# Loading weights one block earlier around the branch mixing of a transformer block

## The chip, the cores and the metric

The kernel runs on one core of a Trainium2 chip. The metric is the device time of one execution in microseconds (us). The kernel computes two transformer blocks over 512 tokens of width 1024, all in float32; this change touches the first block only, between its stick-breaking attention and its first residual addition.

## The reference

What is computed in the part that matters, from `first_block`:

```python
mod = jax.nn.silu(c) @ ada_w[layer] + ada_b[layer]
shift1, scale1, gate1, shift2, scale2, gate2 = [m[:, None, :] for m in jnp.split(mod, 6, axis=-1)]
...
y_a = nsa_attention(...) @ w_up_nsa[layer]                     # 512x512 times 512x1024
y_b = stick_breaking_attention(...) @ w_up_sb[layer]           # 512x512 times 512x1024
mixed = (jax.nn.sigmoid(m_a) * y_a + jax.nn.sigmoid(m_b) * y_b) @ w_out[layer]
h = h + gate1 * mixed
u2 = rms_norm(h, norm2_g[layer]) * (1 + scale2) + shift2
```

`w_up_nsa` and `w_up_sb` (2 MB each) are called the branch weights here, `w_out` (4 MB) the output weight. `ada_w` has 6 x 1024 columns; `gate1`, `scale2`, `shift2` and `gate2` are not computed ahead of this part but beside it.

## The kernel before

The program is a list of blocks. In each `nc.Block()` every engine has its own instruction list; engines meet by semaphores inside a block, and all of them, SyncE (SP) with its DMA issues included, meet in a barrier at its end. SP need not wait for the data of a DMA, only until it has issued it. Scratch memory is a stack from the left (`Scope(nc)`) and one from the right (`beside`).

The blocks around the change, in order:

1. `stick_breaking` (L1366): 8 heads; TensorE, VectorE and ScalarE hand each other the scores. SP has nothing to do in it, and no DMA runs. Its result is in `mT[:, 4:8, :]`, used as `B.oT[1]`.
2. `turn_tokens` with tag `oT` (L2943, function L1509): 4 jobs in which TensorE turns the other branch's output and VectorE (even jobs) or ScalarE (odd jobs) copy it to `oT0`. SP runs `load_up` (L2937): both branch weights into `wu`, units 0 and 1 of the modulation, then two rows of biases (`load_biases`, L154), 512 KB each, one row of 4 KB spread to all 128 partitions.
3. `mix_branches` (L1553): 8 parts, each 128 tokens by 512 columns. A part is 8 matmuls in the code (4 slices of 128 for each of the two branches); the trace has two MATMUL records for each, 16 a part. TensorE starts part i when VectorE has read part i-2 (`read`). VectorE multiplies both banks by the gates `B.sig` (L1593 into `mixed`, L1594 into a scratch tile), GpSimd adds the two (L1607).
4. `turn_tokens` with tag `mT` (L2946): 8 jobs, `mixed` turned into `mT`.
5. `project_residual` (L1610) with tag `o1`: 8 groups of 16 MATMUL records, two halves of `w_out` in `rw0` and `rw1`, both issued by SP at the start of the block (L1634). VectorE multiplies by the gate (L1676), GpSimd adds to `h` (L1693).

The modulation (`class Modulation`, L115) runs inside blocks 3 and 5. It has 8 units of 2 MB of `ada_w`, two buffers `adaw0`, `adaw1`. A unit is: a load (`load_unit`, L162; from unit 2 on it waits until the sum of the unit two before is done), a `sum` on VectorE (1 instruction at L174, 7 at L176, each waiting for the one before), a `spread` on TensorE (2 records at L188 for a gate, 8 at L195 for a scale or shift), and a `finish` on VectorE (L205, L217 or L221 and L222). In `mix_branches` VectorE does unit i//2's `sum` after an even part i and its `finish` after the odd part; TensorE does its `spread` after the odd part, and waits there for the sum. SP issues the loads of units 2 to 5 in `mix_branches`, ScalarE those of 6 and 7 in `project_residual`. Units 4 to 7 are summed in `project_residual`.

Of the kernel before, what the change touches and what calls it, by code (L numbers as in the profile page):

```python
# [22 lines left out]
P = 128  # L23
TOK = 512
NT = TOK // P
D = 1024
# [1336 lines left out]
KEY_OFF = [0, 512, 1024, 896]  # L1363


def stick_breaking(nc, C, B):  # L1366

    with Scope(nc) as s:  # L1370
# [17 lines left out]
            return tile[:, KEY_OFF[b]:KEY_OFF[b] + TOK - P * b]  # L1388

        with nc.Block() as block:  # L1390
            @block.tensor
            def _(pe):
                def scores(n):
                    i, half = n // 2, n % 2
                    r = slice(64 * half, 64 * half + 64)
                    if n >= 2:
                        pe.wait_ge(wgt_ready, 2 * (n - 1))
                    for b in (1, 3, 2, 0):
                        dst = z[half][KEY_BANK[b]][:, KEY_COL[b]:KEY_COL[b] + TOK - P * b]
                        nc.tensor.matmul(dst, B.sbk[r, i, P * b:P * b + P], B.sbq[r, i, P * b:TOK], start=(b != 3), stop=False)  # L1400
                    for b in (1, 3, 2, 0):
                        dst = z[half][KEY_BANK[b]][:, KEY_COL[b]:KEY_COL[b] + P]
                        mm = nc.tensor.matmul(dst, C.ident_r[:, :], C.ban_turned[:, :], start=False, stop=(b != 1))
                        if b != 1:
                            mm.then_inc(z_ready, 1)

                def sums(n):
                    half = n % 2
                    pe.wait_ge(plus_ready, 3 * n + 2)
                    for b in (3, 2, 1, 0):  # L1410
                        if b == 0:
                            pe.wait_ge(plus_ready, 3 * n + 3)
                        bank, col = z[half][KEY_BANK[b]], KEY_COL[b]
                        for a in range(b, NT):
                            first = col + P * (a - b)
                            mm = nc.tensor.matmul(bank[:, first:first + TOK - P * a],
                                                  (C.tri_neg if a == b else C.ones_neg)[:, :], block_of(soft[half], a),
                                                  start=False, stop=(a == NT - 1), skip_group_check=True)
                        if b < 2:
                            mm.then_inc(exponent_ready, 1)  # L1420

                def weigh(n):
                    i, half = n // 2, n % 2
                    pe.wait_ge(wgt_ready, 2 * n + 2)
                    if half == 0 and i >= 2:
                        pe.wait_ge(out_copied, i - 1)
                    for b in range(NT):
                        mm = nc.tensor.matmul(ops[i % 2][64 * half:64 * half + 64, P * b:TOK],
                                              B.sbv[:, b, n * 64:n * 64 + 64], block_of(wgt[half], b),
                                              start=(b == 0), stop=(b == NT - 1), skip_group_check=True)  # L1430
                    mm.then_inc(weighed, 1)

                scores(0)
                scores(1)
                for n in range(0, heads, 2):
                    sums(n)
                    sums(n + 1)
                    for half in range(2):
                        weigh(n + half)
                        if n + 2 < heads:  # L1440
                            scores(n + 2 + half)
# [108 lines left out]
                                         scale=1.0 if scale is None else scale).then_inc(out[1], 1)  # L1550


def mix_branches(nc, B, wu, w_in, mixed, mod):  # L1553


    with Scope(nc) as s:
        tmp = [s.sb(f"mixt{i}", [P, 512]) for i in range(2)]
        ps = [[s.bank(f"mx{i}{b}") for b in range(2)] for i in range(2)]
        ready = s.sem("mx_ready")
        own = s.sem("mx_own")  # L1560
        read = s.sem("mx_read")
        summed = s.sem("mx_sum")
        parts = [(t, n) for n in range(2) for t in range(NT)]
        with nc.Block() as block:
            @block.sync
            def _(sp):
                for u in range(2, 6):
                    mod.load_unit(sp, u)

            @block.tensor  # L1570
            def _(pe):
                for i, (t, n) in enumerate(parts):
                    if i >= 2:
                        pe.wait_ge(read, i - 1)
                    for b in range(2):
                        if i == 0:
                            pe.wait_ge(w_in[b], 16)
                        for k in range(4):
                            mm = nc.tensor.matmul(ps[i % 2][b][:, :], B.oT[b][:, k, P * t:P * t + P],
                                                  wu[b][:, k, 512 * n:512 * n + 512], start=(k == 0), stop=(k == 3))  # L1580
                    mm.then_inc(ready, 1)
                    if i % 2:
                        mod.spread(pe, i // 2)

            @block.vector
            def _(dve):
                ch = Chain(dve, own)
                for i, (t, n) in enumerate(parts):
                    dve.wait_ge(ready, i + 1)
                    dst = mixed[:, t, 512 * n:512 * n + 512]  # L1590
                    if i >= 2:
                        dve.wait_ge(summed, i - 1)
                    ch.link(nc.vector.tensor_tensor(dst, ps[i % 2][0][:, :], B.sig[:, t, 512 * n:512 * n + 512], ALU.mult))  # L1593
                    ch.link(nc.vector.tensor_tensor(tmp[i % 2][:, :], ps[i % 2][1][:, :],  # L1594
                                                    B.sig[:, t, D + 512 * n:D + 512 * n + 512], ALU.mult))
                    dve.sem_inc(read, 1)
                    if i % 2 == 0:
                        mod.sum(dve, i // 2)
                    else:
                        mod.finish(dve, i // 2)  # L1600

            @block.gpsimd
            def _(pool):
                for i, (t, n) in enumerate(parts):
                    pool.wait_ge(read, i + 1)
                    dst = mixed[:, t, 512 * n:512 * n + 512]
                    pool.tensor_tensor(dst, dst, tmp[i % 2][:, :], ALU.add).then_inc(summed, 1)  # L1607


def project_residual(nc, C, aT, w, gate, tag, mod, begun, after, early):  # L1610

# [1 line left out]
    kc = w.shape[0] // P  # L1615
    slots = kc // KD
    with Scope(nc) as s:
        wbuf = [s.sb(f"rw{i}{tag}", [P, KD, 512]) for i in range(2)]
        tmp = [s.sb(f"rt{i}{tag}", [P, 512]) for i in range(2)]
        banks = [s.bank(f"rp{b}{tag}") for b in range(6)]  # L1620
        units = len(mod.units)
        landed = s.sems(f"r_landed{tag}", 2)
        used = s.sem(f"r_used{tag}")
        ready = s.sem(f"r_ready{tag}")
        scaled = s.sem(f"r_scaled{tag}")
# [1 line left out]
        with nc.Block() as block:  # L1627
            @block.sync
            def _(sp):
                for i in range(2 * slots):  # L1630
                    if i >= 2:
                        sp.wait_ge(used, i - 1)
                    n, q = i // slots, i % slots
# [1227 lines left out]
def program(nc, A, out):  # L2861

    Scope.used.clear()
    with Scope(nc) as s:
# [25 lines left out]
        with Scope(nc, "right") as beside, Scope(nc) as s0:  # L2890
# [4 lines left out]
            with Scope(nc) as s1:  # L2895
# [4 lines left out]
                with Scope(nc) as s1b:  # L2900
# [3 lines left out]
                    with Scope(nc) as s2:  # L2904
# [16 lines left out]
                        for tag, kz, branch in (("sl", B.ksz, 1), ("wn", B.kwz, 2)):  # L2921
# [5 lines left out]
                                bias=lambda half, i: C.bias[:, bass.ds(i + 4 * half, 1), :].rearrange("p a n -> p (a n)"),  # L2927
                                gate=lambda half, i: B.ga[:, :, bass.ds(i * 3 + 12 * half + branch, 1)].rearrange("p t a -> p (t a)"),
                                add=True)
                    stick_breaking(nc, C, B)  # L2930
                mod = Modulation(beside, nc, C, M[0], C.cols1, A["ada_w"][0], A["ada_b"][0], [2, 4, 3, 5], "m2")
                with Scope(nc) as s1c:
                    B.oT[0] = s1c.sb("oT0", [P, 4, TOK])
                    wu = [s1c.sb(f"wu{i}", [P, 4, D]) for i in range(2)]
                    w_in = s1c.sems("up_in", 2)

                    def load_up(sp):  # L2937
                        for b, n in enumerate(("w_up_nsa", "w_up_sb")):
                            sp.dma_start(wu[b][:, :, :], A[n][0].rearrange("(k p) n -> p k n", p=P)).then_inc(w_in[b], 16)
                        for u in range(2):  # L2940
                            mod.load_unit(sp, u)
                        mod.load_biases(sp)
                    turn_tokens(nc, C, [(lambda t, k=k: B.oa[:, t, P * k:P * k + P], B.oT[0][:, k, :], None)  # L2943
                                        for k in range(4)], "oT", load_up, back_to_front=True)
                    mixed = s1c.sb("mixed", [P, NT, D])
                    mix_branches(nc, B, wu, w_in, mixed, mod)  # L2946
                    turn_tokens(nc, C, [(lambda t, k=k: mixed[:, t, P * k:P * k + P], mT[:, k, :], None)
                                        for k in range(KD)], "mT")
            project_residual(nc, C, mT, A["w_out"][0], M[0].gate[0], "o1", mod, 4, lambda u: u - 2, 6)
        Scope.clear(nc)  # L2950

        with Scope(nc) as s1:
# [123 lines left out]
```

## Time and profile before

| | us |
|---|---|
| median of 3 runs | 2178.98 |
| lowest and highest of them | 2174.85, 2180.03 |
| the profiled execution | 2174.3 |
| its span | 2172.5 |
| TensorE busy | 1766.9 (81%) |
| VectorE busy | 757.5 (35%) |
| ScalarE busy | 483.4 (22%) |
| GpSimd busy | 219.2 (10%) |

A row of the timeline is: start, length, engine, line of the kernel, instruction, tile written and tiles read, shapes, count, and in brackets how long the engine had been idle before it and what released it. Rows with a count above 1 are merged, and the length is then from the first start to the last end. PE is TensorE's matmul, DVE VectorE, ACT ScalarE, POOL GpSimd; SPq and PEq are the instruction queues of SyncE and TensorE, and "PEq L1515" as a releaser is the barrier that closes a block. A row of the windows is: stretch and its length, busy time with count for PE, PEld, DVE, ACT and POOL, then the mean granted TensorE clock (1.00 is 2.4 GHz, 0.50 is 1.2 GHz), the mean busy share of the DMA engines, and GB/s.

### The profile page before, as it was taken

Reading aid. Unit: us, or ns where it says so; the run is one execution under the profiler, and the core shown is the slowest. Engines: PE = TensorE matmul, PEld = TensorE weight load, DVE = VectorE, ACT = ScalarE, POOL = GpSimd, SP = SyncE. Lnnn points to the kernel's source line nnn. Section 1 sums busy time; section 2 is a strip of 40 time slices with the busy share of each in tenths; the row PEclk is TensorE's granted clock in tenths of the full one; section 3 lists DMA queues with packets and bytes.
Section 4 is the critical chain, followed back from the end, with each engine's and each line's share of the span. In section 5 each row is a group of like instructions: output and inputs, shape, how many; then the busy total and the mean of one; then the engine's idle time right before and its main releaser. Section 6 shows DMA issues by size and latency. Waiting matters only on the chain. (4 is left out here: it accounts for less than half of the span.)

```text
span 2172.5 us, 21463 instructions
## 1 busy us (share of the span) xinstructions
PE 1766.9 (81%) x8022; PEld 1177.2 (54%) x8023; DVE 757.5 (35%) x1353; ACT 483.4 (22%) x804; POOL 219.2 (10%) x261
## 2 busy tenths in 40 slices
PE   4979998887877899899959993688458889988872
PEld 2768876654344678678848881466423233323331
DVE  6334225431544677233351215643231111111113
ACT  3212334432001222222232324242100001100001
POOL 4010001000102122200030000101010000000001
PEclk9989999888989899999979995898568999999997
DMA  9312310002461775222212210004539966799994
GB/s 281 109 58 78 97 40 1 0 0 103 158 223 39 249 252 195 98 77 95 95 43 88 88 58 1 0 25 177 228 149 426 423 265 257 312 426 426 425 424 169
DMA packets 99668, 361.52 MB, mean 166 GB/s; under 512 B 21239, under 2 KB 23459, under 8 KB 87275
## 3 DMA queue, kind: packets, MB, share of 16 engines
q1 hardware_dynamic: 90791, 344.48, 41.8%
q0 software_dynamic: 5760, 9.02, 1.2%
q10 hardware_dynamic: 3012, 6.59, 0.8%
q8 instruction: 69, 1.13, 0.2%
q14 instruction: 36, 0.29, 0.0%
HBM read 357.28 MB, written 14.75 MB: 171 GB/s over the span
## 5 line engine op out<-in xcount | busy, mean ns | idle before, releaser
L2288 PE MATMUL x_gpa<-x_ring,x_Ta 128*64 128x512 f32 x608 | 136.2, 601 | 1.6 <-issue 1.6
L2288 PE MATMUL x_upa<-x_ring,x_Ta 128*64 128x512 f32 x608 | 133.7, 592 | 1.7 <-DMA x_ring<-in_w_expert_up_dram 1.7
L2288 PEld LDWEIGHTS x_gpa<-x_ring,x_Ta 128*64 128x64 f32 x608 | 43.7, 139 | 90.6 <-issue 90.6
L317 DVE TENSOR_TENSOR p_lo<-p_raw,p_hi 128x2048 fp32r<-128x2048 f32 x18 | 41.3, 2292 | 144.9 <-ACT p_hi L670 144.9
L2288 PEld LDWEIGHTS x_upa<-x_ring,x_Ta 128*64 128x64 f32 x608 | 43.6, 137 | 88.9 <-issue 88.9
L324 PE MATMUL fr_p<-p_hi,u_high 128*128 128x512 f32 x224 | 89.1, 398 | 0.0
L2272 PE MATMUL x_t0a<-ident,x_ga 128*128 128x128 f32 x80 | 20.3, 401 | 84.4 <-DMA x_ga<-normed_rows,x_idsa 84.4
L326 PE MATMUL fr_p<-p_hi,u_low 128*128 128x512 f32 x224 | 88.0, 393 | 0.0
L325 PE MATMUL fr_p<-p_lo,u_high 128*128 128x512 f32 x224 | 88.0, 393 | 0.0
L2309 PE MATMUL x_y0a<-x_ring,x_aTa 128*64 128x512 f32 x304 | 78.8, 665 | 1.2 <-ACT x_aTa L2349 1.2
L2309 PE MATMUL x_y1a<-x_ring,x_aTa 128*64 128x512 f32 x304 | 68.4, 592 | 0.0
L2272 PEld LDWEIGHTS x_t0a<-ident,x_ga 128*128 128x128 f32 x80 | 13.4, 207 | 101.0 <-DMA x_ga<-normed_rows,x_idsa 97.7
L670 ACT ACTIVATE p_hi<-p_raw 128x2048 fp32r<-128x2048 f32 (+1 forms) x20 | 37.4, 1872 | 135.5 <-DMA p_raw<-in_w_in_dram 135.5
L176 DVE SCALAR_TENSOR_TENSOR acc1m<-adaw1m,silu_c,acc1m 128x512 f32<-128x512 f32 x70 | 65.4, 934 | 2.5
L2344 ACT ACTIVATE x_siga<-x_gpa 128x512 f32<-128x512 f32 x19 | 11.3, 597 | 243.2 <-PE x_gpa L2288 243.2
L2763 POOL TENSOR_TENSOR hT<-hT 128x512 f32<-128x512 f32 x32 | 48.1, 1502 | 170.1 <-ACT hT L2753 167.3
L2358 DVE TENSOR_TENSOR x_outa<-x_y0a,gates 128x512 f32<-128x512 f32 x19 | 13.1, 691 | 147.4 <-PE x_y1a L2309 147.4
L324 PE MATMUL mp<-uh,w_hi0m 128*128 128x512 f32 x128 | 52.8, 413 | 13.6 <-DVE w_lo0m L317 13.6
L2349 ACT ACTIVATE x_aTa<-x_apa 128x512 f32<-128x512 f32 x19 | 11.3, 597 | 227.5 <-PE x_apa L2296 227.5
L317 DVE TENSOR_TENSOR w_lo0o<-w_raw0o,w_hi0o 128x2048 fp32r<-128x2048 f32 x10 | 22.9, 2292 | 109.9 <-ACT w_hi0o L2810 109.9
L2318 DVE TENSOR_SCALAR x_Ta<-x_t0a,scale,shift 128x128 f32<-128x128 f32 x80 | 27.4, 404 | 84.7 <-PE x_t0a L2272 83.5
L2334 DVE TENSOR_TENSOR x_siga<-x_siga,x_gpa 128x512 f32<-128x512 f32 x19 | 13.1, 687 | 123.0 <-ACT x_siga L2344 123.0
(1007 smaller groups left out, 3997.5 us busy)
## 6 DMA issues: line engine op xcount, KB each, us to landing
x_ring<-in_w_expert_gate_dram SPq DMA_DIRECT2D x32, 2048.0 KB, 23.7
x_ring<-in_w_expert_up_dram SPq DMA_DIRECT2D x32, 2048.0 KB, 18.6
x_ring<-in_w_expert_down_dram SPq DMA_DIRECT2D x32, 2048.0 KB, 21.4
p_raw<-in_w_in_dram SPq DMA_DIRECT2D x18, 1024.0 KB, 5.1
adaw0m<-in_w_ada_dram SPq DMA_DIRECT2D x6, 2048.0 KB, 10.2
adaw1m<-in_w_ada_dram SPq DMA_DIRECT2D x6, 2048.0 KB, 9.7
fr_ada<-in_ada_w_dram SPq DMA_DIRECT2D x4, 2048.0 KB, 17.5
w_raw0m<-in_mlp_w_dram SPq DMA_DIRECT2D x8, 1024.0 KB, 6.6
```

The lines of the kernel that those rows point to most:

```text
L176: ins = v.scalar_tensor_tensor(out=a[:, :], in0=w[:, k, :], scalar=sc[:, k:k + 1], in1=a[:, :], op0=ALU.mult, op1=ALU.add)
L317: return v.tensor_tensor(out, x, high.bitcast(F32), ALU.subtract)
L324: nc.tensor.matmul(ps, ah, bh, start=start, stop=False)
L325: nc.tensor.matmul(ps, ah, bl, start=False, stop=False)
L326: return nc.tensor.matmul(ps, al, bh, start=False, stop=stop)
L670: nc.scalar.activation(hi[i % 2][:, :, 0:n], raw[i % 2][:, :, 0:n], ACT.Copy).then_inc(w_high, 1)
L2272: mm = self.nc.tensor.transpose(self.tps[b][:, P * k:P * k + P], self.xg[:, 4 * b + k::KD], self.C.ident[:, :])
L2288: mm = nc.tensor.matmul(ps[CAP * f:CAP * f + CAP, :], self.xT[:, k, CAP * f:CAP * f + CAP], w[m + f][:, k, :], start=(k == 0), stop=(k == ...
L2309: mm = nc.tensor.matmul(self.yps[n][CAP * f:CAP * f + CAP, :], self.aT[:, k, CAP * f:CAP * f + CAP], w[4 + f][:, 2 * k + n, :], start=(k = ...
L2318: self.nc.vector.tensor_scalar(self.xT[:, k, :], self.tps[0][:, P * k:P * k + P], self.M.scale[1][:, k:k + 1], self.M.shift[1][:, k:k + 1] ...
L2334: ch.link(self.nc.vector.tensor_tensor(self.sig[:, :], self.sig[:, :], self.gps[:, :], ALU.mult))
L2763: pool.tensor_tensor(hT[:, b, :], hT[:, b, :], hT[:, b, :], ALU.mult).then_inc(squared, 1)
```

## The change

The branch weights get a place on the right-hand stack and are issued by SP in the block of `stick_breaking`. The `oT` turn's SP list holds only the two units and the biases. `mixed` is no tile of its own: it is the first half of the gates `B.sig`, so L1593 writes over the gate values that it reads. The room goes to `first_w`, the first half of `w_out`, which SP issues in `mix_branches` right after unit 2's load; `project_residual` takes it as `wbuf[0]` with its semaphore and loads only the second half itself. In `mix_branches` the sum of unit 0 stands ahead of part 0, and those of units 1, 2 and 3 after parts 1, 3 and 5; each `finish` stays after its odd part, now behind the next unit's sum.

```diff
-def stick_breaking(nc, C, B):
+def stick_breaking(nc, C, B, ahead):
...
         with nc.Block() as block:
+            @block.sync
+            def _(sp):
+                ahead(sp)
+
...
-def mix_branches(nc, B, wu, w_in, mixed, mod):
+def mix_branches(nc, B, wu, w_in, mixed, mod, ahead):
...
                 for u in range(2, 6):
                     mod.load_unit(sp, u)
+                    if u == 2:
+                        ahead(sp)
...
                 ch = Chain(dve, own)
+                mod.sum(dve, 0)
                 for i, (t, n) in enumerate(parts):
...
-                    if i % 2 == 0:
-                        mod.sum(dve, i // 2)
-                    else:
+                    if i % 2:
+                        if i < 7:
+                            mod.sum(dve, i // 2 + 1)
                         mod.finish(dve, i // 2)
...
-def project_residual(nc, C, aT, w, gate, tag, mod, begun, after, early):
+def project_residual(nc, C, aT, w, gate, tag, mod, begun, after, early, first_w, landed):
...
-        wbuf = [s.sb(f"rw{i}{tag}", [P, KD, 512]) for i in range(2)]
+        wbuf = [first_w, s.sb(f"rw1{tag}", [P, KD, 512])]
...
-        landed = s.sems(f"r_landed{tag}", 2)
...
-                for i in range(2 * slots):
+                for i in range(1, 2 * slots):
...
-                    stick_breaking(nc, C, B)
+                    wu = [beside.sb(f"wu{i}", [P, 4, D]) for i in range(2)]
+                    w_in = beside.sems("up_in", 2)
+
+                    def load_up(sp):
+                        for b, n in enumerate(("w_up_nsa", "w_up_sb")):
+                            sp.dma_start(wu[b][:, :, :], A[n][0].rearrange("(k p) n -> p k n", p=P)).then_inc(w_in[b], 16)
+                    stick_breaking(nc, C, B, load_up)
...
-                    wu = [s1c.sb(f"wu{i}", [P, 4, D]) for i in range(2)]
-                    w_in = s1c.sems("up_in", 2)
-
-                    def load_up(sp):
-                        for b, n in enumerate(("w_up_nsa", "w_up_sb")):
-                            sp.dma_start(wu[b][:, :, :], A[n][0].rearrange("(k p) n -> p k n", p=P)).then_inc(w_in[b], 16)
+                    first_w = s1c.sb("rw0o1", [P, KD, 512])
+                    first_in = beside.sems("r_landedo1", 2)
+
+                    def load_units(sp):
                         for u in range(2):
                             mod.load_unit(sp, u)
                         mod.load_biases(sp)
+
+                    def load_first(sp):
+                        sp.dma_start(first_w[:, :, :], chunk(A["w_out"][0], 0, 512)).then_inc(first_in[0], 16)
...
-                                        for k in range(4)], "oT", load_up, back_to_front=True)
-                    mixed = s1c.sb("mixed", [P, NT, D])
-                    mix_branches(nc, B, wu, w_in, mixed, mod)
+                                        for k in range(4)], "oT", load_units, back_to_front=True)
+                    mixed = B.sig[:, :, 0:D]
+                    mix_branches(nc, B, wu, w_in, mixed, mod, load_first)
```

## Rows read from the trace of the kernel before

**Rows 1.** Windows: the stick-breaking block, and the four blocks after it.

```profile
425.40:527.50 102.10, 89.82 (x320) 55.71 (x320) 27.65 (x52) 35.77 (x57) 0.00 (x0) 0.86 0.00 1
527.50:692.40 164.90, 131.46 (x360) 64.25 (x360) 76.57 (x104) 3.58 (x6) 20.24 (x16) 0.93 0.44 159
```

**Rows 2.** Timeline, the `oT` turn and the first matmuls of the mixing.

```profile
527.55 0.38 SPq L2939 DMA_DIRECT2D wu<-in_w_up_nsa_dram  x1
...
529.16 8.10 SPq L166 DMA_DIRECT2D adaw1m<-in_ada_w_dram  x1
...
531.44 0.60 ACT L1549 ACTIVATE oT<-tt_ps3oT 128x512 f32<-128x512 f32 x1 [1.19 <-PE tt_ps3oT L1528]
537.30 5.69 SPq L156 DMA_DIRECT2D gates<-in_ada_b_dram  x2
...
543.44 5.14 PE L1579 MATMUL mx<-wu,oT 128*128 128x512 f32 x8 [12.03 <-PEq L1515]
```

**Rows 3.** DMA issues: count, KB each, us from issue to landing.

```profile
wu<-in_w_up_sb_dram SPq DMA_DIRECT2D x1, 2048.0 KB, 12.5
```

**Rows 4.** Timeline, SP's issues at the start of the later `mlp_up` block.

```profile
711.56 0.57 SPq L166 DMA_DIRECT2D adaw0m<-in_w_ada_dram  x1
...
712.89 5.39 SPq L156 DMA_DIRECT2D gates<-in_b_ada_dram  x2
...
720.93 0.48 DVE L174 TENSOR_SCALAR acc0m<-adaw0m,silu_c 128x512 f32<-128x512 f32 x1 [4.23 <-DMA adaw0m<-in_w_ada_dram]
```

**Rows 5.** Timeline, parts 0 to 2 of the mixing.

```profile
548.42 3.60 PE L1579 MATMUL mx<-wu,mT 128*128 128x512 f32 x8
...
552.05 0.69 DVE L1593 TENSOR_TENSOR mixed<-mx,sig 128x512 f32<-128x512 f32 x1 [20.81 <-PE mx L1579]
...
553.62 1.53 DVE L174 TENSOR_SCALAR acc0m<-adaw0m,silu_c 128x512 f32<-128x512 f32 x1
...
555.19 5.47 DVE L176 SCALAR_TENSOR_TENSOR acc0m<-adaw0m,silu_c,acc0m 128x512 f32<-128x512 f32 x7
...
560.72 1.13 PE L188 MATMUL mod_ps0m<-acc0m,ones 128*128 128x512 f32 x2 [1.84 <-DVE acc0m L176]
...
561.68 3.60 PE L1579 MATMUL mx<-wu,oT 128*128 128x512 f32 x8
```

**Rows 6.** Timeline, a spread inside a running stream in `project_residual`.

```profile
643.83 7.03 PE L1653 MATMUL rp2o<-rw0o,mT 128*128 128x512 f32 x16
...
650.69 0.95 PE L195 MATMUL mod_ps0m<-ones,acc0m 128*128 128x1 f32 x8
...
651.50 7.11 PE L1653 MATMUL rp3o<-rw0o,mT 128*128 128x512 f32 x16
```

**Rows 7.** Timeline, end of the mixing, `mT` turn, start of `project_residual`.

```profile
605.83 3.17 PE L1579 MATMUL mx<-wu,mT 128*128 128x512 f32 x7
...
612.25 1.26 POOL L1607 TENSOR_TENSOR mixed<-mixed,mixt 128x512 f32<-128x512 f32 x1 [7.26 <-DVEq L1596]
...
613.97 1.08 PE L1530 MATMUL tt_ps0mT<-ident,mixed 128*128 128x128 f32 x4 [1.62 <-PEq L1564]
...
620.54 0.39 SPq L1634 DMA_DIRECT2D rw0o<-in_w_out_dram  x1
...
628.29 8.83 PE L1653 MATMUL rp0o<-rw0o,mT 128*128 128x512 f32 x16 [8.64 <-DMA rw0o<-in_w_out_dram]
```

**Rows 8.** Windows: granted clock and DMA in idle stretches, the mixing, the `mT` turn, `project_residual`.

```profile
534.70:536.00 1.30, 0.00 (x0) 0.00 (x0) 0.00 (x0) 0.00 (x0) 0.00 (x0) 1.00 0.99 403
...
547.00:552.00 5.00, 5.00 (x13) 2.24 (x12) 0.00 (x0) 0.00 (x0) 0.00 (x0) 1.00 1.05 396
...
613.90:617.40 3.50, 3.43 (x16) 3.46 (x17) 1.29 (x2) 0.60 (x1) 0.00 (x0) 0.50 1.03 369
...
620.50:624.50 4.00, 0.00 (x0) 0.00 (x0) 3.65 (x6) 0.00 (x0) 0.00 (x0) 1.00 0.66 221
...
631.80:689.00 57.20, 56.89 (x145) 25.92 (x143) 19.89 (x29) 0.00 (x0) 8.87 (x7) 1.00 0.22 81
```

More of the change, by code:

```diff
@@ L2942, in load_up @@
                         mod.load_biases(sp)
+                    def load_first(sp):
+                        sp.dma_start(first_w[:, :, :], chunk(A["w_out"][0], 0, 512)).then_inc(first_in[0], 16)
                     turn_tokens(nc, C, [(lambda t, k=k: B.oa[:, t, P * k:P * k + P], B.oT[0][:, k, :], None)
-                                        for k in range(4)], "oT", load_up, back_to_front=True)
-                    mixed = s1c.sb("mixed", [P, NT, D])
-                    mix_branches(nc, B, wu, w_in, mixed, mod)
+                                        for k in range(4)], "oT", load_units, back_to_front=True)
+                    mixed = B.sig[:, :, 0:D]
+                    mix_branches(nc, B, wu, w_in, mixed, mod, load_first)
                     turn_tokens(nc, C, [(lambda t, k=k: mixed[:, t, P * k:P * k + P], mT[:, k, :], None)
                                         for k in range(KD)], "mT")
-            project_residual(nc, C, mT, A["w_out"][0], M[0].gate[0], "o1", mod, 4, lambda u: u - 2, 6)
+            project_residual(nc, C, mT, A["w_out"][0], M[0].gate[0], "o1", mod, 4, lambda u: u - 2, 6, first_w, first_in)
         Scope.clear(nc)
```

## The prediction

> **What bounds the kernel now.** The page's chain of waits only reaches back to 2148 us, so it says nothing of this part; I read the windows first, then the timeline of each block with the idle time in brackets. The windows show that the four blocks from 527.5 to 692.4 us have TensorE busy for 131.5 of 164.9 us, with no other engine above 77 [rows 1]. TensorE is the engine to follow, and what can be won is its idle time, which stands in four places.
>
> Place 1: the barrier that closes the `oT` turn. ScalarE's last copy ends at 531.44 + 0.60 = 532.04 us, but SP issues until 537.30 + 5.69 = 542.99: the fourth 2 MB issue took 8.10 us and the two bias rows 5.69. TensorE starts at 543.44, released by the barrier [rows 2]. The second branch weight, issued right behind the first (527.55 + 0.38 + 0.05), landed 12.5 us later, at 540.5 [rows 3]; so the data would have held the start until 540.5 anyway.
>
> Place 2: three waits inside the mixing. A part is 6.86 us of TensorE (643.83 to 650.69 for the same 16 records) [rows 6]. The sum starts after the even part and runs from 553.62 to 560.66, 7.0 us; it starts 1.8 us after that part ended, so TensorE waits for it before each spread. Part 1's matmuls are through at 548.42 + 3.43 + 6.86 = 558.71, and part 2 starts at 561.68: 2.97 us [rows 5].
>
> Place 3: the tail. The last part is read only after the sum that stands before it on VectorE; from the end of the last matmul, 605.83 + 3.17 = 609.00, to the turn's start at 613.97 it is 4.97 us [rows 7].
>
> Place 4: the first output weight, issued when `project_residual` begins (620.54); TensorE starts at 628.29, released by that DMA [rows 7].
>
> Two cold starts come with it. The first 8 records of the mixing take 4.98 us to the next row's start (543.44 to 548.42, their row is 5.14 against 3.60 for a later 8), 1.55 more than the 3.43 of half a part [rows 2, 5, 6]; the first 16 of `project_residual` show 8.83 against 7.03, 1.8 more [rows 6, 7].
>
> **The change part by part.**
>
> *The `oT` turn.* SP now issues two units and two bias rows. The same four issues, in the same order, stand at the start of `mlp_up`: from 711.56 to 712.89 + 5.39 = 718.28, 6.72 us [rows 4]. So SP is done at 527.55 + 6.72 = 534.27, still behind ScalarE's 532.04, and the mixing starts 0.45 us later (as 542.99 to 543.44) at 534.72: **8.72 us** sooner. Bounds: if nothing blocked, ScalarE would be last and it starts at 532.49 (10.95 sooner); if the third issue blocked for 8.10 and the biases for 5.69 as now, it starts at 527.55 + 0.6 + 13.8 + 0.45 = 542.4 (1.0 sooner). I take the middle value, because the queue holds the same two unit loads there [rows 4]. The branch weights are no wait any more: issued at 425.4 they have 109 us.
>
> *The branch weights during stick-breaking.* Two issues of about 0.4 us on an engine that has nothing else there, and 4 MB in a stretch where no DMA runs (share 0.00) [rows 1]. I take 0. Bounds: nothing gained; at worst every engine stood still while both land, 12.5 us [rows 3]. Beside 396 GB/s [rows 8] the 8 records from 548.42 take 3.60 us, no more than those from 561.68, where the next load had only been issued [rows 5]; the cost of nothing is nearer.
>
> *The sums one part sooner.* Unit 0's load is issued first and lands 9.3 us after issue (711.56 to 720.93, the sum's start) [rows 4], so its sum runs from 536.9 to about 543. Part 0 is then read by 544.5 instead of 542.9; part 2, which waits for that, starts only at 534.72 + 2 x 6.86 + 0.81 = 549.3. Behind it: part 1 read by 551, sum 1 until 558.1 (7.04), finish 0 until 559, part 2 read by 560.5; part 4 needs that at 564. Every later sum has the same 6 us to spare, and the load of unit 2 is issued at about 543, not 560.7. So all three waits go. A spread inside a running stream costs 650.69 to 651.50 = 0.81 us [rows 6]; I take the same for the two records of a gate's. There are three pairs with a part behind them, and 2.97 - 0.81 = 2.16 goes from each: **6.5 us**. Low bound: 0, if something else on VectorE is as late; high bound 3 x 2.97 = 8.9.
>
> *The first matmuls of the mixing.* The granted clock was still 1.00 at 534.7 to 536.0 with TensorE idle after the same turn [rows 8], and TensorE now starts at 534.7. So the 1.55 us of cold start goes: **1.55**, low bound 0.
>
> *The tail.* After the last matmul: 0.05, then L1593, L1594 and the semaphore (552.05 to 553.62, 1.57) [rows 5], L1607 1.26, barrier 0.46: 3.3 us in place of 4.97 [rows 7]. The last spread and finish (0.81, then under 1.3) run beside it. **1.6 us**, bounds 0 and 2.
>
> *`mixed` in place of the gates.* L1593 reads and writes the same 512 columns with the same shapes; nothing later needs these gates. I take 0; if it were twice as long (0.69 more) only the last of eight would be on the path: between -0.2 and 0.7 us.
>
> *The first output weight.* One more SP issue behind unit 2's, at about 544 us; the next, unit 3's, waits for sum 1 at 558. It has over 50 us to land. In `project_residual` TensorE starts with the block: 628.29 - 620.57 = **7.7 us**. What is late next is not VectorE: sums 4 and 5 take 12 us while TensorE needs 20.6 to the first spread, and everything after hangs on TensorE's own progress as now; the second half of the weight has 29 us. The clock was 1.00 at 620.5 to 624.5, before TensorE's start now [rows 8]: **1.8 us** of cold start goes, low bound 0.
>
> *The `mT` turn* may start on a warmer clock, since less idle time stands ahead of it; it now runs at 0.50 for its first 3.5 of 6.6 us [rows 8]. I take 0, between 0 and 2 gained.
>
> Sum: 8.7 + 6.5 + 1.6 + 1.6 + 7.7 + 1.8 = 27.9 us. The profiled execution is 2174.3 us (span 2172.5), so its like would be 2146.4. The median of the runs shown, 2178.98, is 4.7 above it, and I set the prediction against that: 2151. Nothing behind 692.4 us depends on anything but this part's end.
>
> Where a rule speaks otherwise: the `mT` turn consists of transposes only, and its clock rose from 0.50 to full while it ran, to 1.00 in the idle stretch right behind [rows 8]. The Trainium skill (TensorE: Matmul & The Clock Gate, Part 4: PE-mode transpose) says that transposes do not count as TensorE activity and don't bring the full clock. By it the first output matmuls would run at half clock as now, and the sum would lose its last term. This case's trace disagrees.
>
> **The rivals.**
>
> *A, half clock at the start of `project_residual`.* The window above can be one lucky alignment. The last term goes: 26.1 us, 2153.
>
> *B, SP goes on holding the turn.* It decides if the third and fourth issues block as the fourth does now (8.10 + 5.69). Against it stand rows 4. The first term shrinks to 1.0 and the cold start stays: 18.6 us, 2160.
>
> *C, the loads stretch stick-breaking.* A hand-over chain of three engines slowed for up to 12.5 us [rows 3]; half of it is 6: 2157; at most 2163.
>
> *D, the sums don't come off the path:* VectorE's finish now stands behind the next sum, and if that held the read of a part, the 6.5 us would stay: 2157. Against it are the 3.5 us and more of room above.
>
> *E, slower: the clock.* The five blocks lose their idle stretches, and if the chip answered the denser work with 1.2 GHz for long, each record of 0.43 would cost 0.43 more. From 65 records on (27.9 / 0.43) the change loses; one pass of the 128 of `project_residual` at half clock costs 55 us: 2206. Against it: 57.2 us with 56.9 busy ran at 1.00 [rows 8].
>
> **How the numbers follow.** Forecast 0.62 (own range 2147 to 2156, from the unknown turn and tail and the runs' own scatter), A 0.12, B 0.09, C 0.05, D 0.04, E 0.02, and 0.06 for scatter of unrelated stretches, either way. The likeliest gives 2151; the range 2144 to 2160 adds the warmer turn below and reaches B above, and leaves out half of C, E and some scatter. 0.3% is 6.5 us, about what runs of this kernel can tell from no change. Only E and a rare mix of B with C or scatter come to that: faster 0.94, same 0.04, slower 0.02.
>
> **What would show it.** Right: SP's bias rows end within 7 us of the turn's start and the mixing's first matmul follows half a microsecond later; no idle time ahead of any L188 or L195 in the mixing; L1653 starts within 0.1 us of its block, with 7.0 us for its first 16; L1400 to L1428 as long as now. Wrong: a "DVE acc" or "POOL" releaser ahead of TensorE, an adaw issue of several us, stick-breaking longer than 102.1 us, or a granted clock of 0.50 inside the mixing.

## The result and the profile after

The changed kernel takes 2148.94 us in the median (2148.24 to 2149.94, 4 runs) against 2179.51 (2174.85 to 2180.10, 4 runs): the ratio is 0.9873, with a 95% interval of 0.9854 to 0.9892, that is 24 to 32 us less. The profiled execution took 2149.94 us (span 2148.2). The prediction was 2151 us, 27.9 less than before. One execution of all those below, the fourth of experiment 5, took 4189.10 us; no measurement here shows why, and no median, ratio or stage here holds it.

The stages of both profiles, each from its own first matmul to the next stage's (the last to ScalarE's first instruction of the block behind), are read from the timelines:

| stage | before | after | less | forecast |
|---|---|---|---|---|
| stick-breaking | 102.14 | 101.28 | 0.86 | 0 |
| `oT` turn | 15.84 | 7.39 | 8.45 | 8.7 |
| mixing | 70.53 | 62.78 | 7.75 | 6.5 + 1.6 + 1.6 = 9.7 |
| `mT` turn and the wait for the weight | 14.32 | 6.04 | 8.28 | 7.7 |
| `project_residual` | 64.17 | 62.45 | 1.72 | 1.8 |
| together | 267.00 | 239.94 | 27.06 | 27.9 |
| all behind | 1480.04 | 1484.45 | -4.41 | 0 |

The first view of the changed kernel is the timeline of the `oT` turn, to be set beside [rows 2, 4].

```profile
525.04 0.59 SPq L166 DMA_DIRECT2D adaw0m<-in_ada_w_dram  x1
...
526.40 5.63 SPq L156 DMA_DIRECT2D gates<-in_ada_b_dram  x2
...
528.94 0.60 ACT L1553 ACTIVATE oT<-tt_ps3oT 128x512 f32<-128x512 f32 x1 [1.19 <-PE tt_ps3oT L1532]
532.48 5.37 PE L1585 MATMUL mx<-wu,oT 128*128 128x512 f32 x8 [3.58 <-PEq L1519]
535.21 0.49 DVE L174 TENSOR_SCALAR acc0m<-adaw0m,silu_c 128x512 f32<-128x512 f32 x1 [6.47 <-DMA adaw0m<-in_ada_w_dram]
...
537.68 3.60 PE L1585 MATMUL mx<-wu,mT 128*128 128x512 f32 x8
```

SP issues from 525.04 to 532.03, 6.99 us where 6.72 were forecast, and is still the last at the barrier; the mixing follows 0.45 us later. But its first 8 records take 537.68 - 532.48 = 5.20 us, no less than before. The granted clock in windows of the changed kernel (columns as in [rows 8]) tells why:

```profile
531.00:532.40 1.40, 0.00 (x0) 0.00 (x0) 0.00 (x0) 0.00 (x0) 0.00 (x0) 1.00 1.03 360
532.40:535.80 3.40, 3.32 (x5) 1.49 (x6) 0.56 (x2) 0.00 (x0) 0.00 (x0) 0.64 1.02 373
535.80:537.60 1.80, 1.80 (x4) 0.71 (x3) 1.73 (x3) 0.00 (x0) 0.00 (x0) 0.74 1.06 398
```

The clock was still 1.00 when TensorE started, and fell while the first matmuls ran (narrower windows show 0.50 from 533.5 to 536.5 us). The fall came after 3.6 us without work, and the half clock stayed for some 3 us.

The middle of the mixing, parts 1 to 3, to be set beside [rows 5]:

```profile
544.55 3.60 PE L1585 MATMUL mx<-wu,mT 128*128 128x512 f32 x8
547.98 1.02 PE L188 MATMUL mod_ps0m<-acc0m,ones 128*128 128x512 f32 x2
...
548.84 3.60 PE L1585 MATMUL mx<-wu,oT 128*128 128x512 f32 x8
...
551.32 5.47 DVE L176 SCALAR_TENSOR_TENSOR acc1m<-adaw1m,silu_c,acc1m 128x512 f32<-128x512 f32 x7
...
556.71 0.68 DVE L205 TENSOR_TENSOR gates<-mod_ps0m,gates 128x512 f32<-128x512 f32 x1
...
557.62 0.69 DVE L1600 TENSOR_TENSOR sig<-mx,sig 128x512 f32<-128x512 f32 x1 [0.22 <-DVE gates L205]
...
562.57 1.02 PE L188 MATMUL mod_ps1m<-acc1m,ones 128*128 128x512 f32 x2
```

No row of TensorE has an idle time in brackets: the spread costs 0.86 us in the stream (547.98 to 548.84). Part 2 is through at 548.84 + 6.86 = 555.70 and is read 1.9 us late, behind sum and finish; TensorE does not need it before part 4, at 563.43.

The end, to be set beside [rows 7]:

```profile
588.36 3.60 PE L1585 MATMUL mx<-wu,mT 128*128 128x512 f32 x8
...
593.54 1.26 POOL L1614 TENSOR_TENSOR sig<-sig,mixt 128x512 f32<-128x512 f32 x1 [4.27 <-DVEq L1603]
...
595.26 1.08 PE L1534 MATMUL tt_ps0mT<-ident,sig 128*128 128x128 f32 x4 [2.52 <-PEq L1568]
...
601.25 0.39 SPq L1640 DMA_DIRECT2D rw1o<-in_w_out_dram  x1
601.30 7.11 PE L1659 MATMUL rp0o<-rw0o,mT 128*128 128x512 f32 x16 [0.94 <-PEq L1519]
...
608.25 7.03 PE L1659 MATMUL rp1o<-rw0o,mT 128*128 128x512 f32 x16
```

From the last matmul's end (588.36 + 3.60) it is 3.30 us to the turn, as forecast, and TensorE starts with the block. Its first 16 records take 608.25 - 601.30 = 6.95 us, so at full clock from the start. The clock rose inside the turn, which holds nothing but transposes:

```profile
595.20:598.00 2.80, 2.73 (x13) 2.77 (x14) 0.69 (x1) 0.60 (x1) 0.00 (x0) 0.50 0.00 0
598.00:601.00 3.00, 2.36 (x21) 2.13 (x19) 2.08 (x3) 1.79 (x3) 0.00 (x0) 0.97 0.02 5
```

### The profile page after: what moved, and what is told of

Same layout as the page of the kernel before. It is cut to its first block and busy times, and to the rows that moved or that the text cites. A ratio compares the mean times of both kernels' runs of the same rounds, so it can differ in the third digit from the quotient of the medians.

```text
span 2148.2 us, 21463 instructions
## 1 busy us (share of the span) xinstructions
PE 1763.5 (82%) x8022; PEld 1176.5 (55%) x8023; DVE 756.0 (35%) x1353; ACT 483.7 (23%) x804; POOL 219.4 (10%) x261
```

## The experiments

Each is an edit of the changed kernel. A ratio is that to the kernel before, run beside the experiment. Totals scatter by a few us from run to run, so the stages of each profile decide; a stage repeats to 0.1 us where its clock is the same.

**1. The branch weights back in the `oT` turn.**

```diff
-                    stick_breaking(nc, C, B, load_up)
+                    stick_breaking(nc, C, B, lambda sp: None)
...
                     def load_units(sp):
+                        load_up(sp)
```

> The changed kernel with one part undone: the branch weights are issued in the oT turn again, ahead of the units. My theory (SP's issue queue holds the barrier of the turn): the turn takes 15.8 us from its first matmul to the mixing's first instead of 7.4, the mixing starts cold in both, everything else stays, so about 8.5 us more than the changed kernel, 2157.4. Rival (the loads had stretched stick-breaking): stick-breaking gets shorter than the 101.3 us of the changed kernel by some us and so the total rises by clearly less than the turn does. Second rival (the mixing follows the data, not the issue): it starts within 0.5 us of the second branch weight's landing, 12.5 us after its issue, so 2.4 us sooner than SP's last issue allows.

Measured: 2157.42 us (2153.06 to 2162.24), ratio to the kernel before 0.9906 (0.9881 to 0.9931). The turn takes 15.98 us; stick-breaking 101.46. Timeline of that turn, and the landing of the branch weight:

```profile
528.92 8.25 SPq L166 DMA_DIRECT2D adaw1m<-in_ada_w_dram  x1
537.21 5.68 SPq L156 DMA_DIRECT2D gates<-in_ada_b_dram  x2
543.34 6.62 PE L1585 MATMUL mx<-wu,oT 128*128 128x512 f32 x8 [12.17 <-PEq L1519]
```

```profile
wu<-in_w_up_sb_dram SPq DMA_DIRECT2D x1, 2048.0 KB, 12.6
```

The weight issued at 527.74 had landed at 540.3; the mixing waited for SP's last issue, 542.89, as the first theory has it. Both rivals fall. The mixing itself was 1.3 us longer than in the changed kernel (its first 8 records took 6.46 us), since the half clock lasted longer this time: some 6 us from the first matmul, against some 3 in the kernel before, after 12.2 and 12.0 us of idle time.

**2. The old order of the sums.**

```diff
-                mod.sum(dve, 0)
...
-                    if i % 2:
-                        if i < 7:
-                            mod.sum(dve, i // 2 + 1)
+                    if i % 2 == 0:
+                        mod.sum(dve, i // 2)
+                    else:
                         mod.finish(dve, i // 2)
```

> The changed kernel with the old order of sums on VectorE. My theory: idle time of 1.8 us comes back ahead of each of three spreads (2.97 instead of 0.86 us between parts) and the tail from the last matmul to the mT turn is 5.0 instead of 3.3 us: 3 x 2.1 + 1.7 = 8.0 us more, 2156.9. Rival (with all weights there early the order no longer matters, since VectorE has room): under 2 us more.

Measured: 2160.85 us (2159.60 to 2163.22), ratio 0.9930 (0.9907 to 0.9954). The mixing takes 72.47 us, 9.7 more than in the changed kernel; 8.0 were expected. The waits are back at 1.84 us each. The rest is one more cold start (matmuls at half clock behind an idle stretch), after the third of them; timeline and windows of this kernel:

```profile
584.69 1.05 PE L195 MATMUL mod_ps0m<-ones,acc0m 128*128 128x1 f32 x8 [1.84 <-DVE acc0m L176]
...
585.61 5.38 PE L1585 MATMUL mx<-wu,oT 128*128 128x512 f32 x8
```

```profile
584.70:585.60 0.90, 0.90 (x8) 0.90 (x9) 0.86 (x2) 0.00 (x0) 0.00 (x0) 1.00 0.00 0
585.60:588.90 3.30, 3.30 (x7) 1.51 (x7) 1.60 (x3) 0.00 (x0) 1.26 (x1) 0.58 0.85 260
```

5.38 against 3.60 us for the same 8 records. The kernel before had the same three waits and no such fall there. A fourth wait of 1.84 us, ahead of its last spread at 610.84 us, did bring one: that spread took 1.51 us where this kernel's took 1.05. So a wait of 2 us costs 2 us, and now and then 1.8 more when a stream of matmuls follows.

**3. The first half of the output weight issued in `project_residual` again.**

```diff
-                    if u == 2:
-                        ahead(sp)
...
-                for i in range(1, 2 * slots):
+                for i in range(2 * slots):
```

> The changed kernel with the first half of the output weight issued by project_residual again. My theory: TensorE waits 7.7 us for it and then runs its first 16 records at half clock (8.7 instead of 6.95 us): 9.4 us more, 2158.4. Rival (the early load had taken bandwidth from unit 2 and the biases, which held VectorE): the mixing gets shorter than the 62.8 us it takes now, and the total rises by less. Second rival (a restart at full clock after a wait for DMA is possible): only 7.7 us more.

Measured: 2161.1 us (2155.2 to 2166.74), ratio 0.9934 (0.9913 to 0.9956). From the `mT` turn's start to the first output matmul it is 13.93 us (6.04 changed), the first 16 records take 8.38 (6.95), the mixing is 62.79 us in both. That is 7.9 + 1.4 = 9.3 us; both rivals fall.

**4. Four times the load during stick-breaking.**

```diff
+                    again = beside.sem("up_again")
+
+                    def load_often(sp):
+                        for j in range(3):
+                            for b, n in enumerate(("w_up_nsa", "w_up_sb")):
+                                sp.dma_start(wu[b][:, :, :], A[n][0].rearrange("(k p) n -> p k n", p=P)).then_inc(again, 16)
+                            sp.wait_ge(again, 32 * j + 32)
+                        load_up(sp)
-                    stick_breaking(nc, C, B, load_up)
+                    stick_breaking(nc, C, B, load_often)
```

> The changed kernel, the branch weights loaded four times one after the other during stick-breaking, 16 MB in place of 4 (the values are the same). My theory (DMA beside this block costs nothing): stick-breaking takes 101.3 us within 0.8 (its clock rises some us earlier or later), the total stays at 2149 within 2. Rival C (the hand-over chain slows while data lands): if one load costs x, four cost 4x; the prediction's half of 12.5 us would give 18 us more, and even 0.5 us a load would show as 1.5 us in the block.

Measured: 2146.25 us (2144.39 to 2149.97), ratio 0.9858 (0.9836 to 0.9881). Stick-breaking took 103.26 us, so my bound of 0.8 was too narrow: it is 2.0 more than the changed kernel, 1.1 more than the kernel before. The total of 2146.25 is also 0.75 below what I had allowed (2149 within 2). The windows show what the 2.0 us are: first this kernel, then the changed one, each 8 to 12 us and then 28 to 52 us after the block's first matmul.

```profile
433.19:437.19 4.00, 3.25 (x8) 1.46 (x6) 1.14 (x3) 1.26 (x4) 0.00 (x0) 0.50 1.01 407
...
453.19:477.19 24.00, 20.99 (x78) 13.24 (x77) 6.89 (x13) 8.66 (x14) 0.00 (x0) 0.86 0.90 349
```

```profile
431.81:435.81 4.00, 3.25 (x8) 1.46 (x6) 1.14 (x3) 1.26 (x4) 0.00 (x0) 0.50 1.02 409
...
451.81:475.81 24.00, 20.98 (x81) 13.13 (x80) 6.89 (x13) 8.66 (x14) 0.00 (x0) 0.93 0.00 1
```

VectorE's and ScalarE's busy time for the same work is the same to 0.01 us with 349 GB/s beside it and with none (6.89 and 8.66). Only the granted clock differs, 0.86 and 0.93, in a block where TensorE idles now and then. The clock also rose later at the block's start: 19.7 us after the first matmul, against 17.4 in the changed kernel and 18.5 in the kernel before (worked out from the mean granted clock of 16 to 21 us after it). The block's length follows that moment: it is 83.6 to 83.9 us more than it in all thirteen profiles. So rival C's slower engines do not show here. Whether the traffic brought the later rise stays open, since one run cannot tell that from chance.

**5. The bias rows in stick-breaking.**

```diff
+                    bias_in = beside.sem("gb_in_early")
+
+                    def load_early(sp):
+                        load_up(sp)
+                        for m, dst in ((2, M[0].gate[0]), (5, M[0].gate[1])):
+                            sp.dma_start(dst[:, :], rows_to_all(A["ada_b"][0][m * D:(m + 1) * D], D)).then_inc(bias_in, 16)
-                    stick_breaking(nc, C, B, load_up)
+                    stick_breaking(nc, C, B, load_early)
...
+                mod.gb_in = bias_in
...
-                        mod.load_biases(sp)
```

> The changed kernel with the two bias rows issued by SP in stick-breaking, behind the branch weights; the oT turn's SP list holds only the two units. My theory (the mixing starts 0.45 us after the last of SP and ScalarE, and restarts cold because TensorE was idle for 3.6 us, whatever the clock reads at its first matmul): ScalarE's last copy is now last, the turn takes 4.9 us instead of 7.4, TensorE's idle time there is 1.0 us and the first 8 records of the mixing take 3.43 us instead of 5.20: 4.3 us less in all. Rival (the two unit loads alone fill the queue and hold SP as well): the turn stays at 7 us. Second rival (the cold start follows from something else than the idle time before it, such as the DMA traffic): the first 8 records still take 5.2 us, so 2.5 us less.

Measured: 2140.61, 2141.99 and 2145.45 us, ratio 0.9851 (0.9829 to 0.9873). The turn takes 4.75 us and the first 8 records of the mixing 3.51:

```profile
529.14 0.60 ACT L1553 ACTIVATE oT<-tt_ps3oT 128x512 f32<-128x512 f32 x1 [1.19 <-PE tt_ps3oT L1532]
530.04 3.67 PE L1585 MATMUL mx<-wu,oT 128*128 128x512 f32 x8 [0.94 <-PEq L1519]
533.55 3.60 PE L1585 MATMUL mx<-wu,mT 128*128 128x512 f32 x8
```

7.39 - 4.75 = 2.64 and 62.78 - 61.10 = 1.68: 4.3 us, as expected. In stick-breaking SP's row for the two bias issues, right behind the two branch weights, is:

```profile
424.29 1.07 SPq L2947 DMA_DIRECT2D gates<-in_ada_b_dram  x2
```

**6. TensorE kept busy while SP holds the turn.** Three matmuls of 128x512 into a bank of their own, behind the last job, whose result is not used.

```diff
+                for _ in range(warm):
+                    nc.tensor.matmul(spare[:, :], C.flip[:, :], C.ban[:, :], start=True, stop=True)
```

> The changed kernel with three further matmuls of 128x512 whose result nobody reads (2.6 us) behind the last job of the oT turn; SP holds the barrier as long as before, only TensorE's idle time falls from 3.6 to 1.0 us. My theory: the turn takes 7.4 us as in the changed kernel and the first 8 records of the mixing 3.43 us instead of 5.20. Rival: they take 5.2 us.

One run: 2148.06 us. The turn takes 7.40 us, the first 8 records 3.51:

```profile
530.19 2.74 PE L1538 MATMUL tt_spareoT<-ban,flip 128*128 128x512 f32 x6
...
533.94 3.67 PE L1588 MATMUL mx<-wu,oT 128*128 128x512 f32 x8 [1.00 <-PEq L1520]
537.45 2.74 PE L1588 MATMUL mx<-wu,mT 128*128 128x512 f32 x6
```

SP, the barrier and the DMA traffic are as in the changed kernel; only the idle time of TensorE is not. So in this run the cold start hung on that alone.

**7. The bias rows ahead of the units.**

```diff
                     def load_units(sp):
+                        mod.load_biases(sp)
                         for u in range(2):
                             mod.load_unit(sp, u)
-                        mod.load_biases(sp)
```

> The changed kernel with the bias rows issued ahead of the two units in the oT turn. Theory 1 (an issue blocks only when the queue in front of it is full): all four issues take about 0.6 us each, 2.3 in all, ScalarE is last and the turn takes 4.9 us. Theory 2 (a row spread to all 128 partitions takes SP about 5 us by itself, wherever it stands): the first bias row shows 4 to 5 us again and the turn stays at 7.4 us.

One run: 2143.6 us. The turn takes 4.76 us. SP's issues:

```profile
527.75 0.82 SPq L156 DMA_DIRECT2D gates<-in_ada_b_dram  x2
...
528.62 0.59 SPq L166 DMA_DIRECT2D adaw0m<-in_ada_w_dram  x1
...
529.25 0.67 SPq L166 DMA_DIRECT2D adaw1m<-in_ada_w_dram  x1
```

Both bias rows take 0.82 us where they took 5.63 behind the units, and the same four transfers hold SP for 2.2 us in all. So the second theory is out: a bias row is not long by itself, it depends on what is issued ahead of it. That this is a full queue, as the first theory has it, is a reading. The bytes ahead are not the measure: behind the two branch weights, 4 MB like the two units, the rows took 1.07 us (experiment 5). The branch weights move in packets of about 4 KB and the units in packets of about 2 KB (5.24 MB in 1344 packets there, 2.20 MB in 1084 over 525 to 533 us of the changed kernel), so the number of packets may be what counts; no run tested that.

**8. Matmuls at the end of the mixing, alone and with others.** Two of 128x512 whose result is not used, behind the last spread:

```diff
+                pe.wait_ge(read, 7)
+                for _ in range(2):
+                    nc.tensor.matmul(ps[0][0][:, :], B.oT[1][:, 0, 0:P], wu[1][:, 0, 0:512], start=True, stop=True)
```

With the edit of 5:

> As bias_in_stick, and two further matmuls of 128x512 whose result nobody reads, at the end of TensorE's list in the mixing (1.7 us), so that TensorE idles for 1 us instead of 2.5 ahead of the mT turn. My theory: the mT turn starts at full clock and takes 4.6 us to project_residual's first matmul instead of 6.0, so 1.4 us less than bias_in_stick and 5.7 less than the changed kernel. Rival (the first transposes run at half clock however short the idle time is): the turn stays at 6.0 us or gets longer by what the matmuls outlast GpSimd, up to 0.3.

Alone, on the changed kernel:

> The changed kernel with only the two further matmuls of 128x512 at the end of the mixing, whose result nobody reads. Open is whether they or chance gave the 4.63 us of the mT turn in the last run that had them, since a run without them showed 4.62 too. Theory 1 (they keep the clock): 4.6 us. Theory 2 (with 2.5 us of idle time or with 1 us, it is chance where the clock falls): 6.0 to 6.3 us in about every second run of either kind, and so perhaps here.

With the edit of 7:

> The changed kernel with the bias rows issued ahead of the units (SP was free after 2.2 us so) and the two further matmuls at the end of the mixing. By the stages measured one by one: turn 4.76, mixing 61.1, mT turn 4.6, project_residual 62.45, so 5.7 us less than the changed kernel in these stages; in total 5 to 6 less, within the scatter of 3 us of a few runs. Rival (the mT turn's clock is chance): 4.3 less.

Measured: with the edit of 5, 2145.97 us (2144.15 to 2147.48), ratio 0.9859 (0.9842 to 0.9875); alone 2153.28 in its one run; with the edit of 7, 2143.47 us (2139.27 to 2148.49), ratio 0.9852 (0.9832 to 0.9871). The `mT` turn took 4.63, 4.63 and 4.62 us in the three. Without them it took 6.04 to 6.29 in seven profiles and 4.62 in one (experiment 6), with 2.1 to 2.5 us without work ahead of it in all; experiment 3's, which ends in a wait, began at half clock too (0.50 from 595.6 to 598.0 us). With them TensorE idled 0.70 us there. So the clock stayed in three of three with them, and without them it was lost in eight of nine: chance with even odds, as the second theory had it, does not fit well, but three runs leave some room for it. The end of the mixing in the last kernel:

```profile
588.06 0.95 PE L195 MATMUL mod_ps1m<-ones,acc1m 128*128 128x1 f32 x8
...
588.87 1.96 PE L1592 MATMUL mx<-wu,mT 128*128 128x512 f32 x4
591.54 0.63 PE L1534 MATMUL tt_ps0mT<-ident,sig 128*128 128x128 f32 x4 [0.70 <-PEq L1568]
```

From stick-breaking's start to the end of `project_residual` this kernel takes 234.52 us, the changed one 239.94. The totals show no more than experiment 5's alone: the 1.4 us are below what they can tell.

**9. The changed kernel again.**

> The changed kernel once more, to tell its scatter. My theory: the stages from stick-breaking to the first residual repeat to within 1 us (first 8 records of the mixing 5.20, turn 7.4 us), and what differs between executions lies behind them, above all in the expert stage (643.8 to 650.6 us in the profiles so far, with the same instructions). The share of the change that was seen as lost behind it (1484.45 against 1480.04 us) is that scatter, and comes out at another value here. Rival (the change itself costs 4 us later on): the stretch behind takes 1484 us or more again.

Measured: 2148.1 us (2146.27 to 2150.89), ratio 0.9867 (0.9850 to 0.9884). Its stages: 102.04, 7.31, 62.79, 6.19, 62.45; stick-breaking is 0.8 us off the first profile, the others at most 0.15. All behind takes 1483.75 us. This is 0.25 us from what the rival named. But the other ten profiles of kernels with the same instructions there give 1478.9 to 1489.0, among them 1479.32 (experiment 7) and 1480.20 (the last of 8), so the rival's 1484 is no property of the change. The totals leave no room for it either: the ratios 0.9873 and 0.9867 stand for 27.7 and 29.0 us, no less than the 27.06 of the stages. The difference lies in the expert stage for the most part, 643.8 to 650.9 us; the windows of it in the kernel before, then the changed one:

```profile
1502.50:2148.10 645.60, 500.91 (x2259) 213.60 (x2257) 117.55 (x338) 65.67 (x144) 68.44 (x119) 0.87 0.79 330
```

```profile
1475.80:2123.80 648.00, 501.36 (x2250) 212.57 (x2248) 117.56 (x338) 65.52 (x144) 68.55 (x119) 0.87 0.79 329
```

2.4 us more, with the busy time of the matmuls and of the other three engines within 0.5 us (that of the weight loads, which overlap the matmuls, is 1.0 less). What the scatter in this stage comes from stays open.

## Why the prediction was right, and where it was not

*The `oT` turn, 8.7:* measured 8.45. The row it was taken from, the same four issues in a later block (three short issues of L160 stand ahead of them there, which the prediction did not say), was 0.27 us off. Experiment 1 shows that SP's issues held the barrier, and not the landing of the weights, which the prediction had as a second reason 2.5 us below the first. Rival B, the long block of the third issue, did not come; experiments 5 and 7 show that what is issued ahead decides it, and leave open by what measure.

*The branch weights during stick-breaking, 0:* right, and rival C is out: VectorE and ScalarE take no longer, with four times the load either. The 0.86 us that the block was shorter goes with the moment at which its clock rises, 17.4 against 18.5 us after the first matmul; in the changed kernel run again it was 18.4, and the block took 102.04. It takes 101.28 to 102.14 us in twelve of the thirteen profiles, experiment 4's being the other.

*The sums, 6.5:* the three gaps between pairs were 2.97, 2.96 and 2.91 and are 0.86, 0.86 and 0.82, so 6.3. The gate's spread costs 0.86, not the 0.81 taken over from the other kind. The prediction held three waits of 2 us to be worth their length. Experiment 2 shows that removing them also removes a risk: undone, they cost 7.9 us with their tail, as expected, and a cold start of 1.8 on top. Rival D is out: VectorE's read of part 2 was 1.9 us late and nobody waited.

*The first matmuls of the mixing, 1.55:* this term failed; it measured -0.2 (5.20 us against 4.98). The step was "The granted clock was still 1.00 at 534.7 to 536.0 with TensorE idle after the same turn" and "TensorE now starts at 534.7. So the 1.55 us of cold start goes". The clock was indeed 1.00 at the start, but it fell a moment later, behind 3.6 us of idle time that had already passed. The prediction had named a granted clock of 0.50 inside the mixing as a sign of being wrong; it came, and it was this term. Experiments 5, 6 and 7 give the right reading: with 1.0 us of idle time the 8 records take 3.50 or 3.51 us (five profiles of five), with 3.4 to 3.7 us 5.20 or 5.21 (six of six).

*The tail, 1.6:* 4.97 to 3.30, 1.67. *`mixed` in place of the gates, 0:* L1600 takes 0.69 us, as L1593 did.

*The output weight, 7.7 and 1.8:* 14.32 - 6.04 = 8.28, of which 0.6 is the `mT` turn's own clock (5.99 to SP's first issue behind it, 6.57 before; the prediction had left 0 to 2 open), and 8.67 - 6.95 = 1.72. Rival A is out in every profile: the first 16 records took 6.94 or 6.95 us in all eleven that had the weight early. The Trainium skill's rule that transposes don't bring the full clock (TensorE: Matmul & The Clock Gate, Part 4: PE-mode transpose) would have kept these records at half clock; the trace of the changed kernel disagrees as that of before did, with 0.50 and then 0.97 inside a turn of transposes alone. The page's figures there are for bf16, and these transposes are float32.

*Rival E:* the four blocks had TensorE busy for 127.85 of 138.7 us at a mean clock of 0.97, more than before (0.93).

The sum was 27.9; the four blocks gave 26.2. The failed term makes up the difference, and the errors of the others cancel. The totals come as near as they do partly by luck. The medians moved by 30.6 us and the ratio stands for 27.7, where single executions of the kernel before scatter from 2172.69 to 2181.96 us over all comparisons. Of the two profiles the changed one was forecast at 2146.4 us and took 2149.94: the five stages gave 27.06, what stands ahead of them 1.65, and what stands behind took 4.41 back.

## What to carry to other kernels

A block that ends in a barrier ends with its slowest issue, not only its slowest computation: move the loads whose data is needed later into a block where the issuing queue has nothing to do, and issue short transfers ahead of long ones. Here reordering two lines (experiment 7) gave 4.3 us in two stages on top of the 27. And count idle time of TensorE twice: the stretches of 2.1 to 3.7 us here cost themselves and mostly 1.4 to 1.8 us of half clock behind them, which two or three matmuls of no use saved; behind 12 us it cost 1.5 in one kernel and 3.0 in another (4.98 and 6.46 us for 8 records against 3.50).

## What the runs showed of the hardware

- A granted clock of 1.00 at the first matmul after an idle stretch says nothing of the next few us: it fell within the first records, 0.64 over 532.4 to 535.8 us.
- Whether 1.84 us of waiting brings half clock varies: one of four such waits in the kernel before, and one of four in experiment 2.
- The same DMA issue takes SP longer by what is issued ahead of it: two bias rows took 0.82 us first in their block, 1.07 behind the two branch weights and 5.63 behind two units; the second unit took 0.66 us behind one unit and 8.25 with the two branch weights ahead of that as well.
- 349 GB/s of DMA beside a chain of small ScalarE and VectorE instructions left their busy time equal to 0.01 us in 24 us.
